# A hybrid decoder layer on one core: list numbers from one column, two gather pieces moved back, idle products on one tile, two state row groups turned together

## What is computed

```python
h = rmsnorm(x, g_mix)
cv, cg, q, f, v, og, ga, gb = split(h @ w_in)       # 7168 columns
u = cv * sigmoid(cg)                                # 512 channels
full = concat([conv_state, u])                      # 30 old rows ahead
new_conv = full[T:]                                 # last 30 rows: an output
c = silu(layernorm(depthwise_conv31(full) + b))
o, new_state = hgrn2(q, f, v, state)                # 8 heads, 128 x 128
m = (sigmoid(ga) * (c @ w_co) + sigmoid(gb) * (norm(o) * silu(og) @ w_ho)) @ w_o
x = x + m
h = rmsnorm(x, g_ffn)
group = argmax(h @ w_group); two experts of the group's eight, weights `combine`
for e in range(32):
    out += combine[:, e] * ((silu(h @ w_gate[e]) * (h @ w_up[e])) @ w_down[e])
y = rmsnorm(x + out, g_final)
```

## Time and profile before

| | |
|---|---|
| median of 3 runs | 794.11 us (793.79 to 794.77) |
| the profiled execution | 793.69 us, span 791.6 us |
| PE, DVE, ACT, POOL busy | 98%, 30%, 22%, 12% of the span |
| transfers | 265.75 MB, mean 336 GB/s |
| first product of the first pair | 340.05 us |

### The profile page before, as it was taken

One profiled execution on the slowest core, in us unless ns is written; L12 is line 12 of the kernel. 1 busy time (PEld: TensorE's weight loads), 2 busy tenths in 40 slices (PEclk: granted clock), 3 DMA queues, 4 the chain that ended last, 5 costly groups with the idle time before them and its releaser, 6 DMA issues.

```text
span 791.6 us, 10135 instructions
## 1 busy us (share of the span) xinstructions
PE 774.1 (98%) x4140; PEld 435.6 (55%) x4140; DVE 235.6 (30%) x555; ACT 176.5 (22%) x324; POOL 96.4 (12%) x130
## 2 busy tenths in 40 slices
PE   9999999999999999999999999999999989989996
PEld 7888888888888887853333333333333323323322
DVE  4099859473541521441201110111011101101103
ACT  3104332667534301321111011111110010010012
POOL 5200063622400000001001000001000000000001
PEclk9999999999999999999999999999999999999999
DMA  9845576677749995499999999999999999999994
GB/s 335 248 158 184 167 231 201 182 214 187 255 172 328 402 362 203 191 338 421 429 416 414 427 431 425 425 432 425 426 430 426 427 429 427 427 426 420 416 409 164
DMA packets 77480, 265.75 MB, mean 336 GB/s; under 512 B 5551, under 2 KB 37531, under 8 KB 64625
## 3 DMA queue, kind: packets, MB, share of 16 engines
q1 hardware_dynamic: 75490, 261.98, 85.1%
q10 hardware_dynamic: 1479, 1.46, 0.6%
q0 software_dynamic: 464, 1.64, 0.5%
HBM read 258.08 MB, written 7.47 MB: 335 GB/s over the span
## 4 chain that ended last, share of the span: by engine, by line
PE 86%; DMA 9%; issue 2%; DVE 2%; POOL 1%; ACTq 0%; ACT 0%; DVEq 0%; SPq 0%; POOLq 0%
PE bank L2121 25%; PE bank L1694 22%; PE bank L2175 12%; PE bank L1971 7%; PE bank L2183 6%; DMA slot<-in_w_expert_gate_dram 5%; DMA slot<-in_w_expert_up_dram 2%; PE bank L1915 2%; DMA slots<-in_conv_dw_w_dram 1%; PE bank L2068 1%; PE bank L2158 1%; PE bank L2189 1%; PE bank L1726 1%; PE bank L1795 1%; PE bank L2086 0%
## 5 line engine op out<-in xcount | busy, mean ns | idle before, releaser
L1694 PE MATMUL bank<-hT,slots 128*128 128x264 f32 x832 | 189.8, 387 | 0.0
L1694 PEld LDWEIGHTS bank<-hT,slots 128*128 128x128 f32 x832 | 156.6, 190 | 27.1 <-issue 1.0
L2121 PE MATMUL bank<-slots,hT 128*64 128x512 f32 x624 | 168.7, 595 | 1.8 <-DMA slots<-in_w_expert_gate_dram 1.7
L1544 DVE TENSOR_TENSOR x_early<-x_early,bank 128x512 f32<-128x512 f32 (+1 forms) x17 | 11.1, 655 | 333.5 <-PE bank L2121 333.5
L2121 PEld LDWEIGHTS bank<-slots,hT 128*64 128x64 f32 x624 | 52.2, 137 | 91.9 <-issue 87.4
L2175 PE MATMUL bank<-slots,wrep 128*64 128x512 f32 x304 | 85.4, 596 | 0.1
L2121 PE MATMUL bank<-slot,hT 128*64 128x512 f32 x208 | 74.8, 595 | 2.2 <-DMA slot<-in_w_expert_gate_dram 1.6
L2183 PE MATMUL bank<-hT,diag 128*128 128x512 f32 x128 | 64.0, 614 | 0.0
L798 POOL COPY hT<-x_early 128x512 f32 x30 | 17.5, 612 | 367.6 <-PE bank L2121 280.7
L2175 PEld LDWEIGHTS bank<-slots,wrep 128*64 128x64 f32 x304 | 25.9, 137 | 45.7 <-issue 40.8
L1249 DVE SCALAR_TENSOR_TENSOR slot<-slot,rows_buf 128x256 f32<-128x256 f32 x120 | 49.4, 486 | 0.0
(11 more groups left out here) (329 smaller groups left out, 753.3 us busy)
## 6 DMA issues: line engine op xcount, KB each, us to landing
slots<-in_w_expert_down_dram SPq DMA_DIRECT2D x15, 2048.0 KB, 26.1
slots<-in_w_expert_up_dram SPq DMA_DIRECT2D x14, 2048.0 KB, 25.4
slots<-in_w_in_dram SPq DMA_DIRECT2D x13, 2048.0 KB, 9.9
slots<-in_w_expert_gate_dram SPq DMA_DIRECT2D x12, 2048.0 KB, 25.3
slots<-in_w_expert_gate_dram SPq DMA_DIRECT2D x16, 1024.0 KB, 15.8
slots<-in_w_expert_up_dram SPq DMA_DIRECT2D x10, 1024.0 KB, 20.1
slot<-in_w_expert_down_dram SPq DMA_DIRECT2D x5, 2048.0 KB, 30.6
gates<-in_state_hgrn_dram SPq DMA_DIRECT2D x16, 512.0 KB, 5.4
```

The costliest lines, as they stand in the source:

```text
L1544: dve.tensor_tensor(part, part, bank[UP][:, :].rearrange("s (c f) -> s f c", f=FT)[:, fs, :], ALU.mult).then_inc(m_act, 1)
L1694: last = mm(out, w[:, a, t * P:(t + 1) * P], (hT if c else xgain)[:, a, :], start=(a == 0), stop=(a == KT - 1))
L2121: last = mm(out[sl, :], xe[:, a, sl], expert_view(p, kind, e, a // 2)[:, a % 2, :], start=(a == 0), stop=(a == KT - 1))
```

## The change

1. `row_numbers` streams the one column `tok_id[0:m, t:t + 1]`; the numbers of blocks 2 to 4 go to three columns of the bank `GATE`. So they wait for `m_silu` 1, `gather(1)` waits for `list_ready` 2, and `turn(0)` only for `list_ready` 1.
2. `third_piece` and `fourth_piece` stand ahead of products 4 and 6 of `gate(0)` and no longer ahead of 2 and 4. On DVE the two copies are moved back as well, past the slot positions and past `sel1`.
3. POOL makes `ones` first. `keep_busy` multiplies `ones` with `ones`; there are four of them ahead of the gain row and two ahead of the prompt's tokens (two and three before). The wait for `ident` stands ahead of the gain row.
4. `urow` and `usrow` become one item of 38 columns, with four transposes, one copy and the same two stores. All later items of the ring change their bank.

```diff
-        conv_rows = ga[0:30, :, :].rearrange("p a t -> p (a t)")[:, 0:CONV]
-        us_rows = ga[0:NB, :, :].rearrange("p a t -> p (a t)")[:, CONV:2 * CONV]
+        conv_rows = ga[0:30 + NB, :, :].rearrange("p a t -> p (a t)")[:, 0:CONV]
...
-        numbers = bank[4][:, :].rearrange("p (b c) -> p b c", b=len(BLOCKS) - 1)[:, :, 0]
+        numbers, later_numbers = bank[4][:, 0:1], bank[GATE][:, 1:len(BLOCKS) - 1]
...
-            return c_const, ("ident", "ones", "eps", "tri", "score", "wc", "xend", "fold").index(name) + 1
+            return c_const, ("ones", "ident", "eps", "tri", "score", "wc", "xend", "fold").index(name) + 1
...
-        misc_items = ["gain", "rsb", "vec", "taps", "convs", "urow", "usrow"]
+        misc_items = ["gain", "rsb", "vec", "taps", "convs", "urow"]
...
+            pool.memset(ones[:, :], 1.0).then_inc(c_const, 1)
             step(pool.memset(ident[:, :], 0.0))
...
-            pool.memset(ones[:, :], 1.0).then_inc(c_const, 1)
...
-            dve.tensor_copy(conv_rows, src[0:30, :]).then_inc(M_dve, 1)
-            src = take(misc, "usrow")
-            dve.tensor_copy(us_rows, src[0:NB, :]).then_inc(M_dve, 1)
+            dve.tensor_copy(conv_rows, src[0:30 + NB, :]).then_inc(M_dve, 1)
...
-            first_gathered_in(2)
             step(dve.tensor_scalar(live, cm, slot_col[:, :], None, ALU.is_ge))
...
                 if t == 1:
-                    first_gathered_in(3)
+                    first_gathered_in(2)
...
+            first_gathered_in(3)
             dve.wait_ge(m_numbers, 1)
-            dve.tensor_copy(list_at[:, 1:2], numbers[:, 0:1]).then_inc(list_ready, 1)
+            dve.tensor_copy(list_at[:, 1:2], numbers).then_inc(list_ready, 1)
...
-                    mm(bank[0][:, 0:P], ones[:, 0:P], ident[:, :], start=True, stop=True)
+                    mm(bank[0][:, 0:P], ones[:, 0:P], ones[:, 0:P], start=True, stop=True)
...
-            keep_busy(2)
+            keep_busy(4)
             pe.wait_ge(gain_in, 16)
+            pe.wait_ge(*made("ident"))
...
-            keep_busy(3)
+            keep_busy(2)
...
-            turn_rows("urow", 30, lambda c: upad[:, c, SEQ:SEQ + 30])
-            turn_rows("usrow", NB, lambda c: upad[:, c, SEQ + 30:])
+            turn_rows("urow", 30 + NB, lambda c: upad[:, c, SEQ:])
...
-                        last = mm(bank[4][0:n, P * b:P * b + P], sel1[0:m, t, base - P:base - P + n], tok_id[0:m, t:t + 1].broadcast_to([m, P]),
+                        last = mm(bank[GATE if first else 4][0:n, b:b + 1], sel1[0:m, t, base - P:base - P + n], tok_id[0:m, t:t + 1],
...
                     pe.wait_ge(m_act, 1)
+                    pe.wait_ge(list_ready, 2)
...
-                hidden(p, 0, bank[GATE], m_gate, {2: third_piece, 4: fourth_piece} if p == 0 else
+                hidden(p, 0, bank[GATE], m_gate, {4: third_piece, 6: fourth_piece} if p == 0 else
...
-                    pe.wait_ge(list_ready, 2)
+                    pe.wait_ge(list_ready, 1)
...
-                    pe.wait_ge(list_ready, 1)
+                    pe.wait_ge(m_silu, 1)
                     row_numbers(1, len(BLOCKS) - 1)
```

More of the change, by code:

```diff
@@ L751, in conv_sum @@
                 pool.wait_ge(tap_done, CT * TAPS)
-                pool.wait_ge(misc.ready, misc.written("usrow"))
+                pool.wait_ge(misc.ready, misc.written("urow"))
                 tile_sum(conv)
@@ L937, in _ @@
                 if c == 4:
-                    se.wait_ge(*misc.read("usrow"))
-                    se.dma_start(outs["new_conv_prompt"][0, 0], conv_rows).then_inc(conv_stored, 16)
-                    se.dma_start(outs["new_conv_sample"][0, :, TAPS - 2, :], us_rows).then_inc(conv_stored, 16)
+                    se.wait_ge(*misc.read("urow"))
+                    se.dma_start(outs["new_conv_prompt"][0, 0], conv_rows[0:30, :]).then_inc(conv_stored, 16)
+                    se.dma_start(outs["new_conv_sample"][0, :, TAPS - 2, :], conv_rows[30:30 + NB, :]).then_inc(conv_stored, 16)
                 for i in decays.get(c, []):
@@ L1569, in _ @@
                     dve.wait_ge(m_numbers, 2)
-                    dve.tensor_copy(list_at[:, 2:], numbers[:, 1:]).then_inc(list_ready, 1)
+                    dve.tensor_copy(list_at[:, 2:], later_numbers).then_inc(list_ready, 1)
                     for t, (_, m) in enumerate(TOK_TILES):
```

## The result

The changed kernel takes 795.85 us (median of 19 runs, 794.27 to 800.57) against 794.58 us for the kernel before (19 runs beside it; one of these took 3061.43 us and is left out of the ratio as slow). The ratio is 1.002 with an interval of 1.0011 to 1.0028, about 1.6 us (0.9 to 2.2) slower. The forecast was 795.0 in a range of 792.9 to 796.4: the time lies inside, 0.85 above the forecast. Of these 0.85, 0.47 is the kernel before, whose median was 794.11 when the forecast was made. "Within 0.2%" had a chance of 0.64, "slower" 0.23; the ratio stands on the border of the two.

What follows compares the result with a forecast made beforehand. PE was taken to bound the kernel until the first expert pair, then increasingly the weight transfers, started by PE's releases. Head -0.25, state rows -0.44 and gather +1.56 gave +0.87 on 793.69, 794.56; the median adds 0.42: 795.0, range 792.9 to 796.4.

Steps and rivals of the forecast that it cites:

- The stall: In gate(0), PE waits 1.00 us per moved piece for its way through DVE and ACT; +2.3 us in all.
- The fetch is late next: Before gather(1), the row fetch's issue moves by +1.9 us, more than its slack, so PE newly waits for it.
- So the gather starts +1.9 - 0.34 = +1.56 later: At gather(1): the fetch's shift of 1.9 us less its slack of 0.34 delays the gather by 1.56 us.
- the slack: Before gather(1) in the kernel before: the row fetch lands at 361.97, the gather starts at 362.31, 0.34 us later.
- The head: At the kernel's start: ones made first and one idle product less ahead of the prompt's tokens save 0.25 us, bounds 0 and 0.5.
- The rows: At the state rows: four transposes instead of eight save PE 0.44 us, as PE is gapless around them.
- The bank parity changes nothing: At the state rows: items changing bank cost nothing, since each still waits for the one two before it.
- The whole shift reaches the end: From the first expert pair on: PE's delay at the gather passes whole to the end, +1.56 us.
- One-column products: In the row numbers after gate(0): the first group saves 0.4 us, the second 1.0 us.
- No stall: Rival for gate(0): something covers the way through DVE and ACT, the 2.3 us go, end at 792.7; chance 0.10.
- Early release wins: Rival: quarter 2 of gate(0) frees its load 1.3 us earlier and the end follows, 792.1 us; chance 0.10.
- Nothing gained elsewhere: Rival: one-column products and head save nothing, +1.52 us, 795.6; up to 796.3 with longer stalls and fetch; chance 0.25.

Runs made afterwards that it cites:

- e8: The kernel before with the head's change alone (ones first, four and two idle products of ones with ones): 794.2 us, ratio 0.9996.
- f2: The change with its pieces in their old places and the later numbers again as products of 128 columns: 793.93 us, ratio 0.9999.
- e2: The changed kernel with the two pieces and their copies back in their old places: 795.52 us, ratio 1.001.
- f1: The change with its pieces in their old places, plus five idle products in gather(1) before the wait for the row fetch: 794.73 us, ratio 1.0006.
- e5: The change with its pieces in their old places and the gather of block 1 moved behind the down products of pair 0: 797.36 us, ratio 1.003.
- e6: The whole change with the gather of block 1 moved behind the down products of pair 0: 799.18 us, ratio 1.0055.
- f4: The change with its pieces in their old places and the first numbers issued inside gate(0), ahead of product 7: 793.38 us, ratio 0.9992.
- f1-all: The whole change with six idle products of 128 columns in gather(1) ahead of the wait for the row fetch: 795.68 us, ratio 1.0019.
- e4: The kernel before with 38 idle products of 128 columns (8.1 us) ahead of the gate of pair 8: 794.65 us, ratio 1.0004.

## Why the prediction was right, and where it was off

The table gives the shift against the kernel before, in us: of the first product of `gate(0)` (340.05 before), of the gather's start, of SP's issues for the expert weights near 404 and near 761 us, all from the profiles, and of the time (by the ratio).

| kernel | gate(0) | gather | issues near 404 | issues near 761 | time |
|---|---|---|---|---|---|
| the change | +0.30 | +2.49 | +4.17 | +3.28 | +1.6 |
| the change, wait filled | -0.04 | +2.42 | +2.40 | +1.69 | +1.5 |
| pieces alone | +0.57 | +2.80 | +2.79 | +1.69 | +1.3 |
| all but the pieces | +0.29 | -0.05 | +2.92 | +2.61 | +0.8 |
| that, wait filled | +0.08 | +0.22 | +1.16 | +1.57 | +0.5 |
| that, later numbers wide | -0.03 | -0.63 | -0.58 | -0.08 | -0.1 |
| that, numbers ahead of product 7 | -0.32 | -1.63 | -1.58 | -0.49 | -0.6 |

*The stall, right.* Two waits of 1.00 were forecast, 0.94 each came; 12.8 us for `gate(0)`, 12.71 came (353.06 - 340.35), 2.22 more than before where 2.3 was forecast.

*The fetch is late next, right.* A new wait ended by the fetch was forecast and is there, 1.30 us.

*How late, mis-sized.* The step "So the gather starts +1.9 - 0.34 = +1.56 later", with the head's and the rows' 0.69 taken off, gave +0.87; it is +2.49. The parts: POOL's issue moved by +2.30 (354.97 against 352.67), of which the start of `gate(0)` is +0.30, the stalls +2.22 and the first numbers -0.22; the fetch took 9.79 and not 9.3, +0.49; the slack took 0.30. Of the 1.62 between +0.87 and +2.49, 0.99 lies ahead of `gate(0)` (+0.30 and not -0.69), 0.49 in the fetch and 0.2 in the first numbers, which save 0.2 on this chain and not 0.4: their group takes 0.86 where 0.65 was expected; the stalls came out 0.08 smaller. The head was to give 0.25; the point at which PE's records get shorter was assumed to stay, and in this execution it came later, so that the 16 transposes took 3.62 and not 2.84 us (in e8, with the same head, 3.09, and its first real product starts at 8.34 against 8.40 before). By 25 us the head has lost 0.48. That is mostly the execution: the four short records that start at 24.16 in the kernel before start between 24.00 and 25.31 in the nine profiles with the new head (mean 24.49) and between 24.08 and 25.09 in the five with the old one (mean 24.59). So the base of the sum was an execution with an early head, and the 0.25 of the new one isn't to be seen in this spread. The rows were to give 0.44 and gave 0.09, since PE waits 0.35 longer for POOL's sum; that the ring's other bank is the cause isn't shown, but "The bank parity changes nothing" is the sentence that it would overturn.

*The whole shift reaches the end, only partly right.* With 8.1 us it does. With 2 or 3 us a part is taken up: in the change with its wait filled, +2.40 near 404 is +1.69 near 761, and in the pieces alone +2.79 is +1.69. PE's late waits for weights account for half of it: 1.72 + 0.88 + 1.57 = 4.17 us before,

```profile
639.35 7.08 PE L2121 MATMUL bank<-slots,hT 128*64 128x512 f32 x30 [1.72 <-DMA slots<-in_w_expert_gate_dram]
650.22 0.64 PE L2121 MATMUL bank<-x_early,hT 128*64 128x512 f32 x1 [0.88 <-DMA x_early<-in_w_expert_up_dram]
669.66 0.64 PE L2121 MATMUL bank<-slot,hT 128*64 128x512 f32 x1 [1.57 <-DMA slot<-in_w_expert_gate_dram]
```

and 0.82 + 1.17 + 1.55 = 3.54 with the pieces alone: PE comes later, and the weights don't by as much. The other half, 0.49 us, goes while SP issues the next four weight loads back to back: that takes 20.57 us before and 20.08 with the pieces alone. What makes it shorter isn't shown.

```profile
693.07 20.57 SPq L568 DMA_DIRECT2D slots<-in_w_expert_up_dram  x4
```

```profile
695.25 20.08 SPq L568 DMA_DIRECT2D slots<-in_w_expert_up_dram  x4
```

It works the other way too: of the 1.58 that the early numbers gain, 0.49 is left near 761.

So the forecast of +0.87 (795.0) came close to +1.6 partly by luck, with two errors of opposite sign: the gather's shift was 1.6 too small, and some 0.7 to 1.1 of a shift doesn't reach the end.

*One-column products, right in size, without worth.* The second group takes 2.00 us, 1.9 was forecast. In the rule of the Trainium skill, "TensorE: Matmul & The Clock Gate", section "Back-to-back issue gap", few columns cost about 25 ns; the trace has 2.00 / 18 = 0.11 us for a record of one column, and PE's 18 weight loads there take 1.98 us. So the spacing is the weight load's; the same section says of a real stream that the load has a part in it. But PE's 0.9 only lengthened the wait for the fetch: with the second group wide again (f2) the time is 0.9 us less than with it narrow (e2). The intervals of the two ratios overlap, so a loss by the narrow group isn't shown; a gain of its 0.9 us at the end is not there. The difference goes with the clock: none of f2's executions is at 0.993 or less, eight of e2's twelve are, and e2's other four are no slower than f2 (793.60 against 793.93).

*The rivals.* "No stall" fell with the 1.9 us of waits. "Early release wins" fell with the pieces alone, which are slower. "Nothing gained elsewhere", at 795.6 to 796.3, named the right size, and for the head the reason too. It let the rows keep their 0.44 and the stalls be all of the rest; in truth the fetch's own 0.49 and the rows' loss stand in it, and about 0.8 is taken up again.

## What to carry to other kernels

Before work is moved earlier to clear a later engine's queue, write down the way of its result back to the engine that issued it, here 0.93 us through DVE and ACT, and count the work that stands between; with a block of products between there was no stall, with none it was 0.94 us for each piece. Shortening PE's work ahead of a wait buys nothing when a transfer with a slack of 0.34 us is next: move the request for it first, as the kernel with the numbers ahead of product 7 did (gather 1.63 earlier, though its time isn't clear of no change). Read the granted clock of all executions beside their times before a profile's one is taken as typical. And a shift read in the middle of a kernel is worth less at its end where PE later waits for transfers; look for those waits before taking it whole.

## What was not expected of the hardware

- PE went to the lower level of its clock behind some 2 us of one-column products: for 3.4 us in f1, with PE busy all the while, for 3.4 us in the change, where a wait of 1.30 us lay between, and for 6.8 us in e2 and e5, with waits of 1.04 and 0.67 us. It did not from 356 to 370 us in three other profiles with the same products (e6, f4, f1-all). So one profile can carry 1.7 us by chance.
- Twelve of the fourteen profiles have 3.4 us at the lower level near 700 us too, each right behind a wait of PE of 2.55 to 3.40 us; two (e4, e8) have none, with waits of 3.05 and 2.42 us in the same place. A long wait comes before the lower level most times, and is neither enough nor needed.
- Where PE's pace doubles in the head differs between executions of kernels with the same head: the 16 transposes took 3.00, 3.13 and 3.62 us in three of them, and the products of 264 columns right behind them 411 (mean of three) or 647 ns. The granted clock reads 1.00 there in all of them, so this is read off the records' length only.
- The fetch of list rows took 8.9 to 10.1 us from issue to landing in the fourteen profiles, a spread larger than the slack that it had.
